# Branch gates by seven half products with the tokens standing, and the first weight sum made by an adding DMA

## The reference, cut to what matters

```
h = rmsnorm(x, mix_pre_g)
proj = h @ w_in                      # 2048 x (2048 + 1024 + 4096)
a_in, b_in, gates = split(proj)      # 2048, 1024, 4096 columns
a = silu(layernorm(causal_conv(a_val * sigmoid(a_gate), 31 taps)))
y_a = a @ w_a_out                    # 1024 x 2048
mixed = per-group map of (trailing means of b_in minus b_in)   # 1024 -> 1024
y_b = (mixed * pool_scale) @ w_b_out # 1024 x 2048
g_a, g_b = split(sigmoid(gates))
merged = g_a * y_a + g_b * y_b
x = x + rmsnorm(merged @ w_o, mix_post_g)
```

## Time and profile before

| | us |
|---|---|
| median of 3 runs (2543.63 to 2546.49) | 2544.37 |
| span of the profiled execution | 2544.4 |
| PE busy | 2498.3 (98%) |
| DVE busy | 1922.4 (76%) |
| ACT busy | 1053.4 (41%) |
| POOL busy | 193.7 (8%) |
| mean granted clock of PE | 0.994 |

### The profile page before, as it was taken

The page is one execution under the profiler, slowest core; times in us unless marked ns, Lnnn a source line. Parts: engine busy times, 40 slices in busy tenths (PEclk is TensorE's granted clock), DMA queues, the critical chain, the costliest instruction groups (busy, mean ns, idle before and its releaser), DMA issues. The chain is left out here.

```text
span 2544.4 us, 35985 instructions
## 1 busy us (share of the span) xinstructions
PE 2498.3 (98%) x14180; PEld 2193.4 (86%) x14180; DVE 1922.4 (76%) x2289; ACT 1053.4 (41%) x1224; POOL 193.7 (8%) x273
## 2 busy tenths in 40 slices
PE   9999999999999999999999999999999999999998
PEld 7788888888888787899999999999987878877886
DVE  7888766653335788889989998899988787788434
ACT  5222322252224445444444444444454453455323
POOL 0000000000000000011111111011111111200000
PEclk9999999999999999999999999999999999999999
DMA  4322333234334564467777776777787777976221
GB/s 170 106 101 91 100 99 99 91 123 134 99 99 148 166 216 181 152 196 207 211 187 213 215 218 204 195 207 210 222 269 238 262 237 192 278 228 226 89 99 67
DMA packets 155602, 435.48 MB, mean 171 GB/s; under 512 B 13504, under 2 KB 49344, under 8 KB 154432
## 3 DMA queue, kind: packets, MB, share of 16 engines
q1 hardware_dynamic: 120400, 304.12, 34.4%
q0 software_dynamic: 32656, 124.80, 20.3%
q10 hardware_dynamic: 2400, 4.53, 0.5%
HBM read 396.44 MB, written 36.96 MB: 170 GB/s over the span
## 5 line engine op out<-in xcount | busy, mean ns | idle before, releaser
L1259 ACT ACTIVATE w_hi<-ring_raw 128x1024 fp32r<-128x1024 f32 x426 | 450.6, 1060 | 606.6 <-PE ps L1144 388.0
L1762 DVE TENSOR_TENSOR ring_lo<-ring_raw,w_hi 128x1024 fp32r<-128x1024 f32 x426 | 518.6, 1222 | 190.5 <-ACT w_hi L1259 188.5
L873 PE MATMUL ps<-xg_hi,w_hi 128*128 128x512 f32 x1024 | 401.3, 392 | 7.7 <-DVE w_lo L1721 4.1
L1721 DVE TENSOR_TENSOR w_lo<-w_raw,w_hi 128x1024 fp32r<-128x1024 f32 x160 | 195.1, 1223 | 282.5 <-ACT w_hi L1239 282.3
L874 PE MATMUL ps<-xg_lo,w_hi 128*128 128x512 f32 x1024 | 399.6, 390 | 0.0
L875 PE MATMUL ps<-xg_hi,w_lo 128*128 128x512 f32 x1024 | 399.6, 390 | 0.0
L1142 PE MATMUL ps<-s_hi,w_hi 128*128 128x256 f32 x1280 | 362.3, 283 | 2.4 <-issue 2.4
L1144 PE MATMUL ps<-s_hi,ring_lo 128*128 128x256 f32 x1280 | 362.5, 283 | 0.0
L1143 PE MATMUL ps<-s_lo,w_hi 128*128 128x256 f32 x1280 | 362.1, 283 | 0.0
L1239 ACT ACTIVATE w_hi<-w_raw 128x1024 fp32r<-128x1024 f32 x160 | 168.8, 1058 | 390.3 <-PE ps L875 353.9
L1142 PE MATMUL ps<-xg_hi,w_hi 128*128 128x256 f32 x960 | 271.2, 282 | 0.6 <-DVE ring_lo L1762 0.6
(11 more groups left out here) (284 smaller groups left out, 4360.8 us busy)
## 6 DMA issues: line engine op xcount, KB each, us to landing
ring_raw<-in_w_up SPq DMA_DIRECT2D x200, 512.0 KB, 4.7
ring_raw<-in_w_down SPq DMA_DIRECT2D x114, 512.0 KB, 4.5
w_raw<-in_w_in SPq DMA_DIRECT2D x110, 512.0 KB, 3.2
ring_raw<-in_w_up POOLq DMA_DIRECT2D x80, 512.0 KB, 5.9
out_raw<-in_w_o SPq DMA_DIRECT2D x48, 512.0 KB, 4.2
ring_raw<-in_w_ple_gate SPq DMA_DIRECT2D x32, 512.0 KB, 3.5
xd_raw<-gx_dram POOLq DMA_DIRECT2D x14, 1024.0 KB, 10.6
gx_dram<-g_sums POOLq DMA_DIRECT2D x44, 256.0 KB, 7.9
```

Source lines behind the costliest of these rows:

```text
L873: pe.matmul(o, w_hi[:, s, cols], hi, start=start, stop=False)
L1259: f(w_hi[:, (U_S + n) % SLOTS], raw_of(n), ACT.Copy).then_inc(hi_ready, 1)
L1721: dve.tensor_tensor(w_lo[:, s], w_raw[:, u.slot(RAW)], as_f32(w_hi[:, s]), ALU.subtract).then_inc(lo_ready, 1)
L1762: dve.tensor_tensor(low_of_unit(n), raw_of(n), as_f32(w_hi[:, (U_S + n) % SLOTS]), ALU.subtract).then_inc(lo_ready, 1)
```

## The change

The gates leave the tiles of M1 and M2 and get a stage of their own between stage B and the branches. The list `MIX` holds 114 units for them and the map, then 32 for the branches:

- The 4096 gate columns are four pairs of groups of 512 (`GATE_COLS`). Each pair is made by seven products over halved channels and halved tokens, 4 units each. The tokens stand, 512 weight columns move; a unit is 12 matmuls. In pair 0 the map's two units come after the four units of `W11`.
- The products need four sums of quadrants of the scaled input (`xs_hi`, `xs_lo`): ACT scales x in place during stage B (`scale_x`), DVE makes the sums there (`x_sum`), ACT and DVE their highs and lows early in pair 0 (`x_sum_high`, `x_sum_low`).
- Weight sums: `T1` by an adding DMA from POOL (`add_first`), `T2` and `T3` by POOL's own `tensor_tensor`, `T4` by DVE.
- The products are combined by DVE (`gate_second`, `gate_first`, `gate_fourth`, `gate_third`, `gate_other`, 128x1024 each), put through the sigmoid by ACT with the token factor as scale, and stored to DRAM (`gate_store`). POOL brings them back for the branches (`gates_back`).
- The mapped pooling result goes to DRAM and back too (`map_store`, `mixed_raw`), since its buffer is needed for the x sums.
- Three chunks of convolution taps are spread over the gate units, one tap per unit.
- The branches: 2 sides x 4 column groups x 4 units, tokens standing, 24 matmuls a unit. The product with the gates is in token rows (`mtok`), and 16 transposes per group on PE (`turn_branch`) bring `merged` back to channels on partitions. Before the first branch unit the ring of raw buffers has 8 places, after it 6 (`MIX_HOME`); a place is loaded again when PE has done the unit in it.
- Many semaphores are shared between stages, with their counts moved along.

The diff, cut to its core (indents shortened). The first two pieces are common tables; then come SP, POOL, PE, ACT and DVE:

```diff
+def gate_units(h):
+    if h == 0:
+        units = [(GATE, h, W11, q) for q in range(4)] + [(POOLED, n) for n in range(2)]
+        units += [(GATE, h, W21, q) for q in range(4)] + [(GATE, h, mat, q) for q in range(4) for mat in (T1, T2, T4)]
+    else:
+        units = [(GATE, h, mat, q) for q in range(4) for mat in ((W11, T1, T2, T4) if q < 3 else (W11, T2, T1, T4))]
+        units += [(GATE, h, W21, q) for q in range(4)]
+    return units + [(GATE, h, mat, q) for q in range(4) for mat in (T3, W22)]
...
+MIX = [unit for h in range(GATE_GROUPS) for unit in gate_units(h)]
+N_GATES = len(MIX)
+MIX += [(BRANCH, side, n, v) for side in range(2) for n in range(NG) for v in range(BRANCH_UNITS)]
+N_MIX = len(MIX)
+MIX_AT = {unit: j for j, unit in enumerate(MIX)}
+MIX_HOME = [j % GATE_RING if j < N_GATES else (j - N_GATES) % BRANCH_RING for j in range(N_MIX)]
+MIX_BEFORE = [max((i for i in range(j) if MIX_HOME[i] == MIX_HOME[j]), default=None) for j in range(N_MIX)]
...
+if MIX[j][0] == GATE:
+    _, h, mat, q = MIX[j]
+    return w_gates[0 if mat in (W11, T1, T3) else 1, q, GATE_COLS[h][0 if mat in (W11, W21, T4) else 1]]
+if MIX[j][0] == POOLED:
...
+def mix_free(j):
+    home, before = MIX_HOME[j], MIX_BEFORE[j]
+    if before is not None:
+        sp.wait_ge(units_done, U_M + before + 1)
+    elif home < RAW:
+        sp.wait_ge(lo_ready, U_M - 1 + home)
+    elif home < RAW + SLOTS:
+        sp.wait_ge(units_done, U_M - SLOTS + home - RAW + 1)
+    else:
+        sp.wait_ge(pooled_ready, HC)
...
+def gate_landed(h, mat, q):
+    j = MIX_AT[GATE, h, mat, q]
+    pool.wait_ge(mix_in[MIX_HOME[j]], mix_landed(j))
+    return mix_raw[MIX_HOME[j]][:]
+def add_first(h, q):
+    to = gate_landed(h, T1, q)
+    pool.dma_start(to, w_gates[0, q, GATE_COLS[h][0]], accum_op=ALU.add).then_inc(first_gate_added[q], 16)
+def gate_sums(h, q):
+    first = gate_landed(h, T1, q)
+    pool.wait_ge(first_gate_added[q], 16 * (h + 1))
+    second = gate_landed(h, T2, q)
+    pool.tensor_tensor(second, second, first, ALU.add).then_inc(gate_sum, 1)
+add_first(0, 0)
+for _, h, mat, q in (unit for unit in MIX if unit[0] == GATE):
+    if mat == T4:
+        gate_sums(h, q)
+        if q < 3:
+            add_first(h, q + 1)
+    if mat == T3:
+        third = gate_landed(h, T3, q)
+        pool.tensor_tensor(third, third, gate_landed(h, W22, q), ALU.add).then_inc(gate_sum, 1)
+        if h < GATE_GROUPS - 1 and q == 3:
+            add_first(h + 1, 0)
+for k in range(2):
+    pool.wait_ge(mixed_out[k], 16)
+pool.wait_ge(units_done, U_M + MIX_AT[GATE, GATE_GROUPS - 1, W21, 3] + 1)
+pool.dma_start(mixed_raw[:], mixed_dram).then_inc(mixed_in, 16)
...
+def gate_bank_free(h, mat):
+    before = GATE_TAKEN * (h - 1)
+    if mat == W21:
+        pe.wait_ge(gate_copied, h + 1)
...
+    pe.wait_ge(gate_taken, before + GATE_TAKEN_AT[{W11: T4, T2: T3, T4: W22}[mat]])
+if h == 0 and mat in (T1, T2, T3, W22):
+    pe.wait_ge(xs_split, {T1: 1, T2: 2, T3: 3, W22: 4}[mat])
...
+def gate_unit(j):
+    _, h, mat, q = MIX[j]
+    if q == 0:
+        gate_bank_free(h, mat)
...
+def turn_branch(n):
+    pe.wait_ge(mtok_ready, BLK * (n + 1))
+    for q in range(4):
+        for b in range(BLK):
+            mm = pe.transpose(ps[:, 4 * (n % 2) + q, b * P:(b + 1) * P], mtok[:, n, b, q * P:(q + 1) * P], ident[:])
+    mm.then_inc(mtok_turned, 1)
...
+def mix_split(j):
+    kind, h, mat, q = (*MIX[j], None, None)[:4]
+    if kind == GATE and mat == T1:
+        act.wait_ge(first_gate_added[q], 16 * (h + 1))
+    elif kind == GATE and mat in (T2, T3):
+        act.wait_ge(gate_sum, gate_summed(h, mat, q))
+    elif kind == GATE and mat == T4:
+        act.wait_ge(fourth_gate_sum, 4 * h + q + 1)
+    else:
+        act.wait_ge(mix_in[MIX_HOME[j]], mix_landed(j))
+    f(mix_hi(j), mix_raw[MIX_HOME[j]][:], ACT.Copy).then_inc(hi_ready, 1)
...
+def x_sum_high(k):
+    half, tok = ((upper, far), (lower, near), (lower, far), (upper, near))[k]
+    if half == lower:
+        for n in range(2):
+            act.wait_ge(mixed_out[n], 16)
+    act.wait_ge(xs_ready, 4)
+    f(xs_hi[:, half, tok], xt_raw[:, half, tok], ACT.Copy).then_inc(xs_hi_ready, 1)
...
+def gate_sigmoids(h, k):
+    if k == 0:
+        act.wait_ge(gate_out[0], 16 * h)
+        src = by_halves(gate_pair(h, W21))
+    else:
+        act.wait_ge(gate_taken, GATE_TAKEN * h + {2: 4, 3: 5, 1: 6}[k])
+        src = gate_part(k)
...
+def gates_after(j):
+    for h in range(GATE_GROUPS):
+        near_done, end = MIX_AT[GATE, h, W21, 3], MIX_AT[GATE, h, W22, 3]
+        if j == MIX_AT[GATE, h, W11, 3]:
...
+if j == near_done:
+    gate_sigmoids(h, 0)
+if j == near_done + 1:
+    gate_store(h, 0)
+last = h == GATE_GROUPS - 1
+if j == end + 1:
+    gate_sigmoids(h, 2)
+if j == end + (1 if last else 2):
...
+def mixed_high(k):
+    act.wait_ge(mixed_in, 16)
+    f(mixed_hi[:, 2 * k:2 * k + 2], mixed_raw[:, 2 * k:2 * k + 2], ACT.Copy).then_inc(mixed_hi_ready, 1)
...
+def mix_split(j):
+    kind, h, mat, q = (*MIX[j], None, None)[:4]
+    raw = mix_raw[MIX_HOME[j]]
+    if kind == GATE:
+        if mat == T2:
+            fourth = MIX_AT[GATE, h, T4, q]
+            dve.wait_ge(gate_sum, gate_summed(h, T2, q))
+            dve.wait_ge(mix_in[MIX_HOME[fourth]], mix_landed(fourth))
+            to = mix_raw[MIX_HOME[fourth]]
+            dve.tensor_tensor(to[:], to[:], raw[:], ALU.add).then_inc(fourth_gate_sum, 1)
+        if mat == T1:
+            dve.wait_ge(gate_sum, gate_summed(h, T2, q))
+        if mat == W22:
+            dve.wait_ge(gate_sum, gate_summed(h, T3, q))
+    dve.wait_ge(hi_ready, U_M + j + 1)
+    dve.tensor_tensor(mix_lo[MIX_HOME[j]][:], raw[:], as_f32(mix_hi(j)), ALU.subtract).then_inc(lo_ready, 1)
...
+def x_sum_low(k):
+    half, tok = ((upper, far), (lower, near), (lower, far), (upper, near))[k]
+    dve.wait_ge(xs_hi_ready, k + 1)
+    low(xs_lo[:, half, tok], xt_raw[:, half, tok], xs_hi[:, half, tok], xs_split)
...
+def gate_third(h):
+    dve.wait_ge(units_done, U_M + MIX_AT[GATE, h, T3, 3] + 1)
+    dve.wait_ge(gate_taken, GATE_TAKEN * h + 3)
+    third = by_halves(gate_pair(h, T3))
+    dve.tensor_tensor(gate_part(2), gate_part(2), third, ALU.subtract).then_inc(gate_taken, 1)
+    dve.tensor_tensor(gate_part(3), third, gate_part(1), ALU.add).then_inc(gate_taken, 1)
...
+end_of_map, tap = MIX_AT[POOLED, 1], 0
+for j in range(N_GATES):
+    step(At(U_M + j))
+    for k, at in enumerate((end_of_map + 2, end_of_map + 3, end_of_map + 9, end_of_map + 11)):
+        if j == at:
+            x_sum_low(k)
...
+    if j >= N_GATES - 4:
+        mixed_low(j - N_GATES + 4)
+    elif j >= end_of_map + 4 and tap < 3 * CONV_W:
+        conv_taps(HC // 2 + 1 + tap // CONV_W, tap % CONV_W, tap % CONV_W + 1)
+        tap += 1
+for tap in range(tap, 3 * CONV_W):
+    conv_taps(HC // 2 + 1 + tap // CONV_W, tap % CONV_W, tap % CONV_W + 1)
 op.settle()
 dve.tensor_scalar(acc[:], acc[:], 1.0 / H, None, ALU.mult).then_inc(mean_sum_ready, 1)
...
+def gated(side, n):
+    dve.wait_ge(gates_in[2 * side + n % 2], 16 * (n // 2 + 1))
+    for b in range(BLK):
+        if b < BLK - 1:
+            dve.wait_ge(branch_blocks, 3 * (NG * side + n) + b + 1)
+        else:
+            dve.wait_ge(units_done, U_Y + BRANCH_UNITS * (NG * side + n + 1))
+        gates, src = gate_in[2 * side + n % 2][:, b], ps[:, branch_bank(side, n, b)]
+        if side == 0:
+            dve.tensor_tensor(mtok[:, n, b], src, gates, ALU.mult).then_inc(tiles_taken, 1)
```

More of the change, by code:

```diff
@@ L204, in landed @@
 def landed(n):
-    return 16 * sum(loads(m) for m in range(n + 1) if SLOT[m] == SLOT[n])
+    before = 1 + MIX_HOME.count(SLOT[n]) + OUT_HOME.count(OUT_SEM.index(SLOT[n])) if SLOT[n] < O_RING else 0
+    return 16 * (before + sum(loads(m) for m in range(n + 1) if SLOT[m] == SLOT[n]))
 def added(n):
-    return 16 * sum(adds(m) for m in range(n + 1) if SLOT[m] == SLOT[n])
+    before = 0 if SLOT[n] > O_RING else 1 if 4 <= SLOT[n] < O_RING else 4
+    return 16 * (before + sum(adds(m) for m in range(n + 1) if SLOT[m] == SLOT[n]))
 def sums_made(n):
@@ L1010, in branch @@
-            def branch(u, t, hi, lo, arrives=None, ahead_of_branch=None, within_gate=None, gate=True):
-                if gate:
-                    tile(u, t, xg_hi, xg_lo, between=within_gate)
-                if ahead_of_branch:
-                    ahead_of_branch()
-                tile(u + 2, t + 1, hi, lo, chunks=HC, arrives=arrives)
-            for m in range(4):
-                branch(At(U_M1 + 3 * m), At(T_M1 + 2 * m), mixed_hi, mixed_lo, gate=m > 0, arrives=mixed_ready if m == 0 else None)
@@ L1033, in variance @@
                 for b in range(BLK):
-                    mm = pe.matmul(ps[:, 4, b:b + 1], acc[:, b * P:(b + 1) * P], ones[:, 0:1], start=True, stop=True)
+                    mm = pe.matmul(ps[:, 6, b:b + 1], acc[:, b * P:(b + 1) * P], ones[:, 0:1], start=True, stop=True)
                 mm.then_inc(sums_done, 1)
-            for m in range(12, DC):
```

(9 more changed lines are left out.)

671 lines of the change are left out of this document (427 added, 244 removed).

## The result

The changed kernel takes 2567.85 us, the kernel before, run beside it, 2545.28: a ratio of 1.0097, 95% interval 1.0082 to 1.0111. It is 22.6 us slower. I had put no change, 2545, first; the measured time lies outside that case's own range (2535 to 2556) and at the very end of the range that I gave 8 in 10 (2518 to 2568).

The account below looks back on a forecast made before the run. TensorE, busy 98% of the span, was taken as the bound, the stage as pure matmul issue. 2544.4 - 36.0 + 10.4 + 4 + 13.3 + 9.3 = 2545 us; own range 2535 to 2556, 8-in-10 range 2518 to 2568.

Parts of the forecast that it names:

- PE work: TensorE: 192 fewer gate matmuls, -43.5 us; added transposes +7.0 and small sums +0.5; net -36.0.
- Front: Start of the stage: PE waits before the map, T1 and T2, plus a clock tail; +10.4 us, between 2 and 16.
- Inside the four pairs: Gate pairs: T1's chain and DVE's load both covered; +4 us for head-of-line waits, bounds 0 and 72.
- the forecast's case: The summed steps, Pool sums not slowing DVE: 2545 us, own range 2535 to 2556, chance 0.45.
- Rival B: Gate pairs: Pool and DVE stop each other, each Pool sum taking 2.26 us out of DVE; 2561 us, chance 0.25.
- The chain: Gate pairs: T1's load, adding DMA, Pool's sum and low take 14.8 of 19.0 us, hidden; pair 0 late 0.8 a round.
- Rival C: Gate pairs: the adding DMA is the bound, landing in 10.7 us; 2585 us, chance 0.08.
- End of the gates: Gates to branches: late first branch load, then PE waits for the mean behind DVE's queue; +13.3 us, between 5 and 18.
- Gates back from DRAM: Branches: late gate reads hold up group 1's third block, plus clock tail and squares' chain; +9.3 us, between 0 and 16.
- After the stage: Output projection: last transposes hide in its first two units, and its large DVE work starts later; 0 us.

Follow-up runs that it names:

- one-input edit: Changed kernel with each of GpSimd's 32 sums replaced by an in-place multiplication by 1.0, one tensor read in place of two; 2559.27 us.
- Turning the buffers: Changed kernel with the branch units' buffers turned by two, so the first branch units are loaded earlier; 2560.57 us.
- the kernel with the short landing: Changed kernel with T1's adding DMA cut to 64 of its 1024 columns, GpSimd's 32 sums kept; 2554.24 us.
- The three fastest kernels: Changed kernel without GpSimd arithmetic, plus eight scheduling edits; T3's sums by adding DMA 2534.82 us, half by DVE 2531.78, all by DVE 2538.10.

## Why the prediction failed, step by step

The stage took 560.3 us (275.5 to 835.8) against 535.8 - 36.0 = 499.8 of pure work, so 60.5 are waits, lower clock and unplaced; I had written 37. The list, with the clock's loss read from windows of 20 us below 1.00:

- **PE work, -36.0: right.** The count of matmuls and their pitch came out as said.
- **Front, +10.4: 8.1.** Idle before the map 2.65, before T1 2.12, before T2 1.54 (said: 2.0, 2.2, 3.5), and 1.8 of lower clock. The places are right, and so is the list: PE starts T2 at 319.4, where I had 318.9.
- **Inside the four pairs, +4: 33.5. This is the step that failed.** Idle 24.75 (12.1 in pair 0) and 8.8 of lower clock (0.88 in 330 to 350, 0.77 in 350 to 370, 0.91 in 610 to 630). I had set idle over 15 us in the pairs as what would refute the forecast. Three parts of it:
  - *Pool's sum beside DVE.* I priced it as 2.26 us inside a chain and at nothing for DVE, in the forecast's case. It takes 2.34 at the shortest, above the upper bound that I gave it, and 2.7 to 2.9 on average. From DVE it takes 45 x 0.294 + 42 x 0.226 + 101 x 0.082 = 31.0 us in the taps and lows, and 4.2 more in the three additions to `acc` (2.10 on average, alone 0.69). That is 35 us over 32 sums, 1.1 each. Rival B had this, with "decides from 1.7 us per sum"; the mean is below that, and B's own 2.26 was too large. The one-input edit still gives back time.
  - *The chain.* I had it 14.8 of 19.0 long and hidden. Its add lands in 7.9, not 6.7, its sum takes 2.7, and both come again before the next add can start: in pair 0 the sums start at 305.22, 317.88, 329.41 and 339.94, a round of 10.5 to 12.7 where 8.2 were there (I had 9.0). DVE, in order, stood 39.3 us behind those sums with lows and bank reads queued after them. I took "the head start covers most" without walking DVE's queue. Rival C is the same place with a dearer landing; the 10.7 it needed did not come.
  - *DVE's order in pair 0.* T3's first unit takes the bank of T1 one unit (2.7 us) after T2 ends, and two bank reads of 1.2 stand behind a low. I had left this wait out. With no Pool sums it is still 2.9.
  
  The cross-check is the kernel without Pool sums: in the pairs it has 3.2 us of idle time and 1.8 of lower clock, 5.0 in all. My +4 would have done for a kernel whose Pool sums cost nothing.
- **End of the gates, +13.3: 10.1.** The idle at the first branch matmul is 4.86 (said 4.5); then came 1.63 and 1.82 (said 6.1), and 1.8 of clock. My list of DVE's queue was right: it had the mean ready 16.0 us after the last gate matmul, and PE makes it at 653.47, which is 16.0 after 637.4. Turning the buffers gave back some 7, so the named cause holds.
- **Gates back from DRAM, +9.3: 4.9.** The wait for group 1's third block is 0.51 where I had 4.3; the wait behind the squares is 2.79 (2.3), clock 1.6. Pool issued the reads 30.1 us after the last gate matmul (I had 31.1), and group 0's gates were there after 5.3 where I had 9.5. DVE stood 8.0 us waiting for them, and PE hardly felt it.
- **After the stage:** the output projection lost a further 2.2 (26.1 late at the feed-forward part's first matmul), and the down projection and what follows gave back 3.8. I had said 0 for both.

What lies outside these is 3.9. So 8.1 + 33.5 + 10.1 + 4.9 + 3.9 = 60.5, and 60.5 - 36.0 = 24.5. By the first instruction of the output projection the kernel is 23.9 late (0.6 lies in where the stage's ends are read), and 23.9 + 2.2 - 3.8 = 22.3, the difference of the spans.

The three other waits came out 9.9 us smaller in all than I had them, and that hid a third of the 29.5 by which the pairs were missed. Part of it is an error that worked in my favour. My lists say when an operand is ready. To the wait for it I added 2.7 for a lower clock; but slow matmuls ahead of a wait only shorten it, so in the front and at the end of the gates that loss was counted twice. The 2.7 was misread too: 0.89 over 30 us is 6.6 us at the lower level, 3.3 lost. In the stage one fall of the clock cost 1.7, or 3.4 at pair 0's two long waits.

The Trainium skill's page SBUF — State Buffer, section Who interferes with whom, was the warning, and in kind it is borne out: instructions with two inputs in SBUF were stretched, and those that read one bank and one tile were not (seven of them ran beside a Pool sum and took 1.21 to 1.23). The section has the later one of two wait in full. Here the longest low was 3.42 and the longest tap 2.91, each 2.2 more than alone, nearly a whole Pool sum, so for a sum with two inputs the trace agrees; beside a Pool multiplication of 2.76 with one input a low took 2.05 at most, 0.8 more, and there it does not. The mean over all sums was 1.1, because DVE was often waiting for that very sum: in the kernel with the short landing, where it waits only 5.6 us for the sums, the lows and taps alone lose 1.5 a sum. The estimate of 2.25 for the sum, from the Trainium skill's GPSIMD Engine Reference, section 3.1, was low: 2.34 was the shortest measured.

## What to carry to other kernels

A sum given to an engine that is "free" is not free if another engine must wait for it or is slowed while it runs: walk the in-order queue of the engine that consumes the result, instruction by instruction, before calling a chain hidden. When a resource recurs in a loop (add, sum, next add), compare the length of the round with the period, not the length of the chain with the lead. When a list says at what moment an operand is ready, a slower clock ahead of that moment is already in it. The three fastest kernels have no Pool sums; theirs are divided between adding DMAs and DVE, each made when its input has landed. Of the divisions, the one with half of T3's sums on each was fastest, clear of the one with all on DVE and not clear of the one with all by DMA.

## What the runs showed of the hardware

- A Pool 128x1024 fp32 sum of two SBUF tiles takes 2.34 to 2.40 us at the shortest and up to 3.88 beside DVE. A DVE instruction with two tiles that meets one goes from 1.22 up to 3.42 or from 0.75 up to 2.91; reads of one bank and one tile stay at 1.21 to 1.23. One tile in SBUF is not always safe: in the kernel with the short landing two of three `tensor_scalar` taps met a Pool sum and took 1.56 and 2.59 where 0.54 is usual.
- A Pool multiplication by a constant of the same tile, one input, is slower (2.76 us at the shortest), but stretches DVE by 0.8 only: the longest low was 2.05 and the longest tap 1.53. I had expected either no effect or the full one.
- Adding DMAs of 512 KB from GpSimd's queue land in 7.2 to 8.5 us in this stage (medians), against 3.8 for one of 32 KB. Plain loads beside them land in 4.3 to 4.5 with 16 adds, in 4.9 with 24 and in 5.4 to 5.7 with 32.
